# Second routed layer of a two-block network: sixteen raw slots with eight rounded halves, and identity products in three waits of TensorE

## The reference, cut to what matters

```
logits = (x @ w_router); top_val, top_idx = lax.top_k(logits, 2)
top_w = jax.nn.softmax(top_val)
for e in range(8):
    h = silu(x @ w_gate[e]) * (x @ w_up[e])          # 1024 -> 3584
    y = y + gate[..., e:e + 1] * (h @ w_down[e])     # 3584 -> 1024
```

## Time and profile before

| | |
|---|---|
| median of 3 runs | 2169.67 us (2169.33 to 2169.8) |
| profiled execution | 2166.96 us, of which the span is 2165.2 us |
| TensorE busy | 93% of the span |
| VectorE busy | 58% |
| ScalarE busy | 46% |
| DMA queue of SyncE | 571.56 MB, 69.9% of the 16 engines' span |

### The profile page before, as it was taken

How to read it: one execution, slowest core, us unless ns; L and a number is a source line. 1 busy time by engine, 2 the same in 40 slices (tenths; PEclk the granted TensorE clock), 3 DMA queues, 4 the chain that set the end, 5 groups by cost and what they waited for, 6 DMA issues and landing times.

```text
span 2165.2 us, 29319 instructions
## 1 busy us (share of the span) xinstructions
PE 2011.4 (93%) x11542; PEld 1494.7 (69%) x11542; DVE 1256.7 (58%) x1928; ACT 996.9 (46%) x1406; POOL 162.4 (8%) x151
## 2 busy tenths in 40 slices
PE   8998899999898898999989799999999999999996
PEld 7996885434497688998867676656755675575785
DVE  4557652222446677667366766646744674574797
ACT  3554442111143644443375546436644564463773
POOL 2103100000000012342000000000000000000000
PEclk9998998999999999999999989999999999999998
DMA  8650529999764125656711579999999999999994
GB/s 270 191 176 1 165 94 393 416 418 418 273 212 155 46 82 188 196 179 175 199 40 60 194 273 413 408 410 402 412 408 414 412 396 412 412 413 407 409 401 169
DMA packets 228362, 601.32 MB, mean 278 GB/s; under 512 B 16091, under 2 KB 121967, under 8 KB 205568
## 3 DMA queue, kind: packets, MB, share of 16 engines
q1 hardware_dynamic: 220112, 571.56, 69.9%
q0 software_dynamic: 8112, 27.91, 4.1%
HBM read 594.37 MB, written 5.05 MB: 277 GB/s over the span
## 4 chain that ended last, share of the span: by engine, by line
PE 70%; DMA 11%; DVE 10%; ACT 6%; issue 2%; POOL 0%; SPq 0%; DVEq 0%; ACTq 0%
PE psF L1425 8%; PE psF L1427 8%; PE psF L1426 8%; PE psB L1425 7%; PE psB L1426 7%; PE psB L1427 7%; DMA ring<-in_moe_w_up_dram 4%; PE psF L1881 4%; PE psB L2062 2%; DMA ring<-in_moe_w_gate_dram 2%; DVE ring_rounded L3486 2%; PE psB L1905 2%; DMA ring<-in_moe_w_down_dram 2%; PE psF L2062 2%; PE psB L1746 2%
## 5 line engine op out<-in xcount | busy, mean ns | idle before, releaser
L3486 DVE TENSOR_TENSOR ring_rounded<-ring,arena_rounded 128x1024 fp32r<-128x1024 f32 x296 | 350.1, 1222 | 168.2 <-ACT arena_rounded L2649 160.8
L2649 ACT ACTIVATE arena_rounded<-ring 128x1024 fp32r<-128x1024 f32 x296 | 302.6, 1057 | 196.3 <-DMA ring<-in_moe_w_gate_dram 144.0
L2926 DVE TENSOR_TENSOR ring_rounded<-ring,ring_rounded 128x2048 fp32r<-128x2048 f32 (+1 forms) x68 | 147.1, 2165 | 155.5 <-ACT ring_rounded L2376 155.3
L1426 PE MATMUL psF<-ring_rounded,arena_rounded 128*128 128x512 f32 x560 | 222.5, 397 | 0.0
L2376 ACT ACTIVATE ring_rounded<-ring 128x2048 fp32r<-128x2048 f32 (+1 forms) x71 | 128.6, 1815 | 82.1 <-PE psF L1427 62.8
L1425 PE MATMUL psF<-arena_rounded 128*128 128x512 f32 x352 | 143.6, 408 | 11.6 <-DVE ring_rounded L3486 8.5
L1427 PE MATMUL psF<-arena_rounded 128*128 128x512 f32 x352 | 140.3, 399 | 0.0
L1426 PEld LDWEIGHTS psF<-ring_rounded,arena_rounded 128*128 128x128 f32 x560 | 106.9, 191 | 22.0
L1425 PE MATMUL psB<-yT_rounded,ring_rounded 128*128 128x256 f32 x384 | 110.5, 288 | 3.8 <-DVE ring_rounded L2926 2.8
L1426 PE MATMUL psB<-memT_rounded,ring_rounded 128*128 128x256 f32 x384 | 109.2, 284 | 0.0
L1427 PE MATMUL psB<-yT_rounded,ring_rounded 128*128 128x256 f32 x384 | 109.1, 284 | 0.0
(11 more groups left out here) (577 smaller groups left out, 4836.9 us busy)
## 6 DMA issues: line engine op xcount, KB each, us to landing
ring<-in_moe_w_gate_dram SPq DMA_DIRECT2D x224, 512.0 KB, 9.0
ring<-in_moe_w_up_dram SPq DMA_DIRECT2D x224, 512.0 KB, 10.0
ring<-in_moe_w_down_dram SPq DMA_DIRECT2D x112, 1024.0 KB, 9.6
ring<-in_w_dram SPq DMA_DIRECT2D x48, 1024.0 KB, 16.4
arena<-in_w_dram SPq DMA_DIRECT2D x16, 1024.0 KB, 18.8
ring<-in_w_in_dram SPq DMA_DIRECT2D x14, 1024.0 KB, 5.4
ring<-in_ff_w_gate_dram SPq DMA_DIRECT2D x11, 1024.0 KB, 7.3
ring<-in_ff_w_up_dram SPq DMA_DIRECT2D x11, 1024.0 KB, 9.8
```

Source lines behind the costliest of these rows:

```text
L1426: mm(bank, x1, w2, start=False, stop=False, skip_group_check=open_groups)
L2649: ap_(piece(idx, w_hi).bitcast(R32), piece(idx, raw_halves), ACT.Copy).then_inc(piece_high, 1)
L2926: V.tensor_tensor(ring_r[:, slot_of[c], 0:kt * w].bitcast(R32), raw, ring_r[:, hi_slot[c], 0:kt * w], ALU.subtract).then_inc(weights_low, 1)
L3486: V.tensor_tensor(piece(idx, low_halves).bitcast(R32), piece(idx, raw_halves), piece(idx, w_hi), ALU.subtract).then_inc(piece_low, 1)
```

## The change

The ring of raw pieces gets four more half slots, in the memory of `memT` and `mv`, so 16 in all. The rounded high halves go down from 12 to 8, all in `arena`. A load waits for the piece 16 before it; the first four loads to the new slots wait for `ln8 transposed`, after which nobody reads that memory. ScalarE waits before each rounding, from the ninth big piece on, until the eighth big piece before it has been used. The new slots use four semaphores of the ordinary weight ring again, with its counts added. In three waits of TensorE at the beginning of the layer it repeats an identity product of 256 columns into bank F[3]: 4 times before the picks, 2 times before the gathered rows are saved, 6 times after they are turned.

```
-HALF_SLOTS = 2 * RING
+HALF_SLOTS = 2 * RING + 4
+HIGH_SLOTS = 8
...
+        self.big_at = [idx for idx, b in enumerate(self.pieces) if b]
...
-        raw_halves, low_halves = [ring[:, i] for i in range(RING)], [ring_r[:, i] for i in range(RING)]
+        raw_halves = [ring[:, i] for i in range(RING)] + [v[:].rearrange("p a b -> p (a b)") for v in (memT, mv)]
+        low_halves = [ring_r[:, i] for i in range(RING)] + w_hi[4:6]
...
-        piece_in = [sem(f"piece_in{i}") for i in range(HALF_SLOTS)]
+        piece_in = [sem(f"piece_in{i}") for i in range(2 * RING)] + w_in[0:4]
...
+        def landing(idx):
+
+            slot, count = order.landed[idx]
+            return piece_in[slot], count + (landed[slot - 2 * RING] if slot >= 2 * RING else 0)
...
         def piece(idx, memory):
 
+            if memory is w_hi:
+                return half_slot((order.big_no[idx] - 1) % HIGH_SLOTS, w_hi)
             return half_slot(idx % HALF_SLOTS, memory)
...
                     if idx >= HALF_SLOTS:
                         sp.wait_ge(piece_used, idx + n - HALF_SLOTS)
-                    elif idx % 2 == 0:
+                    elif idx % 2 == 0 and idx < 2 * RING:
                         sp.wait_ge(*freed[held_before[layer.first + idx // 2]])
+                    elif idx == 2 * RING:
+                        sp.wait_ge(proj_saved, saved("ln8 transposed"))
...
-                    slot, count = order.landed[idx]
-                    pe.wait_ge(piece_in[slot], count)
+                    pe.wait_ge(*landing(idx))
...
+                stay_warm(F[3], 4)
                 pe.wait_ge(tokens_halved, 1)
                 pe.wait_ge(first_picked, 1)
...
                     ins.then_inc(first_gathered, 1)
+                stay_warm(F[3], 2)
                 pe.wait_ge(first_saved, 2)
                 turn_x(0)
+                stay_warm(F[3], 6)
...
-                            slot, count = order.landed[idx]
-                            act.wait_ge(piece_in[slot], count)
+                            act.wait_ge(*landing(idx))
+                            if order.big_no[idx] > HIGH_SLOTS:
+                                act.wait_ge(piece_used, order.big_at[order.big_no[idx] - 1 - HIGH_SLOTS] + 1)
                             ap_(piece(idx, w_hi).bitcast(R32), piece(idx, raw_halves), ACT.Copy).then_inc(piece_high, 1)
```

## The result

The changed kernel takes 2157.41 us (median of 4 runs, 2152.63 to 2158.46), the kernel before on the same chip 2169.74 us. The ratio is 0.994, with an interval of 0.9923 to 0.9957. Further down, the median of eighteen slots with the changed end and those of the kernel before on its chip (2168.06) hold one slow execution each (3952 and 3344 us), which the ratios leave out.

What follows compares the result with a forecast made beforehand. The layer was taken as bound by one full stream of loads with a hole at its start. Slots (5.5 us for pair 28/29) plus products (2.8) gave 8.3 us: 2169.67 to 2161.4 us, own range 2160.6 to 2163.3, 8-in-10 range 2158 to 2166.5.

Steps and rivals of the forecast that it cites:

- the identity products: TensorE's early waits: fillers hold the clock for the gate part, gaining 2.8 us; the clock still falls after find_tokens.
- All uses come 2.8 us earlier: TensorE from piece 7 on: uses come 2.8 us earlier, so the loads gain this besides the slots' lead.
- Four more slots: SyncE's loads at the layer's beginning: four go out early, later ones wait 16 back; pair 28/29 goes 5.5 us earlier.
- The price of the products: TensorE's early waits: fillers cost nothing, 0.232 us each at full clock; even at half clock overrun at most 0.1 us.
- The gate part: TensorE, first gate part: all 48 matmuls at the faster step take 11.3 us instead of 14.2.
- Eight high halves: ScalarE's roundings: waiting for the big piece 8 back costs nothing and adds no busy time.
- The rival that ended slower: Big steps: eight halves too few, TensorE waits 2.2 us in each of 20, 2176.5 us; chance 0.08.
- Idle fillers: Layer's beginning: fillers do not hold the clock, only the slots' lead of 5.4 us remains, 2164.3 us; chance 0.18.
- Unused lead: After the beginning: TensorE can't use the stream's lead, only 2.8 us arrive, 2166.9 us; chance 0.08.
- The longer lead: Load stream's beginning: gather and loads no longer meet, or the hole nearly closes; lead 11 us, 2158.7 us; chance 0.06.
- Gaps of TensorE from too few buffers: Whole layer: twelve slots cause TensorE's 28.9 us idle, four more remove up to all of it, 2140.8 us; chance 0.02.
- The conversion to a median: Total: the runs' median lies 2.7 us above the profiled execution, so 2169.67 - 8.3 = 2161.4 us.

Runs made afterwards that it cites:

- eighteen slots with the changed end: Changed kernel with 18 raw slots, 6 high halves, no products before the gather, three at the end, VectorE's last subtractions split around the turned rows: 2152.15 us, ratio 0.9929.
- four high halves: Changed kernel with 20 raw slots and 4 high halves, ScalarE rounding four pieces, not six, ahead of the first gathered rows: 2161.42 us, ratio 0.9969.
- the mixed find_tokens: Changed kernel without identity products, the 28 narrow matmuls in four groups between gate pieces and behind the first up piece: 2160.06 us, ratio 0.996.
- products only: Kernel before, with twelve slots and twelve high halves, plus the identity products at the three places: 2162.42 us, ratio 0.9968.
- products at the end: Changed kernel plus six identity products in TensorE's wait ahead of the last down part: 2159.12 us, ratio 0.9957.
- no first products: Changed kernel without the four identity products ahead of the gather: 2158.26 us, ratio 0.9955.
- eighteen and six: Changed kernel with two of the eight high halves given to the raw slots, 18 raw and 6 high: 2153.26 us, ratio 0.994.
- slots alone: Changed kernel without the three groups of identity products, so sixteen slots and eight high halves: 2164.08 us, ratio 0.9977.

## Why the prediction was nearly right, and where it fell short

The mechanism held, and one of its terms was too small. A load issued earlier at the beginning is worth its whole time at the end: the lead of pair 28/29 and that of the last rows agree within 1.6 us in all kernels but three, which have a reason of their own (four high halves, the mixed find_tokens, the changed end), and slots and products add up. TensorE was less ahead than the stream at first and caught up by having less idle time, as forecast.

**The step that failed** is in the identity products: it was said there that `find_tokens` "still lets the clock fall after it", "and that is not removed". I had priced the products by the gate part alone, 2.8 us. That part gave 2.1 in this profile (it ends 33.96 us after the anchor for 36.07) and 2.8 in products only. But with the products the clock also stayed full through and behind `find_tokens`, and that gave 3.1 more. The use of piece 13 can be read from the load that waits for it: pair 24/25 before, 1276.29 - 1225.60 = 50.69 us after the anchor, and pair 28/29 after, 45.47. That is 5.2 us earlier, not 2.8. So the term "All uses come 2.8 us earlier" was mis-sized by 2.4 us, and the pair's lead with it: 5.5 + 5.2 = 10.7, where 5.5 + 2.8 = 8.3 was forecast. With 10.7 in the sum the forecast would have been 2159.0 us, inside the range; the last 1.6 us down to 2157.41 have no cause that a run shows, and the second measurement of the same kernel, 2160.39, lies inside the range. So that the first fell outside it is in part scatter.

Nor is the 3.1 us certain in each execution. In the second profile of the changed kernel the fall was there, if shorter, and the use of piece 13 led by 50.69 - 46.73 = 4.0:

```profile
1268.00:1272.00 4.00, 4.00 (x12) 3.19 (x11) 3.40 (x3) 0.54 (x1) 2.81 (x2) 0.58 0.38 94
```

It was there too in the kernel with products at the end, whose beginning is the same:

```profile
1268.00:1272.00 4.00, 4.00 (x14) 3.15 (x13) 2.83 (x3) 0.00 (x0) 2.25 (x2) 0.67 0.39 84
```

**Four more slots**: 5.5 forecast, 5.4 measured alone. Right.

**The price of the products** was wrong by a factor of two. "10 in 2.32 us" are five products, since each of these fp32 products is two instructions. "Even the slow case overruns by no more than 0.1 us" was therefore false for the first group: the gather began 1.1 to 1.5 us later in the profiles where that group started in time (14.40 to 14.78 us after the anchor for 13.28), and 2.3 us later in the first. How much of this reaches the gate part isn't shown; it began 0 to 0.6 us later. That a faster gather gains nothing was right: the gate part begins at 21.89 us with the gather at half clock (no first products) and at full clock (eighteen and six).

**The gate part**: begun at full clock, 11.5 us, forecast 11.3.

**Eight high halves** cost nothing that a median can show, and six left the lead of 14.2 us whole. The rival that ended slower needs 1.9 us a step; in the changed kernel ScalarE's idle time ahead of roundings that is put down to TensorE is under 4 us in the whole layer.

**The other rivals.** Idle fillers: excluded, the clock was 1.00. Unused lead: excluded by slots alone. The longer lead of 11 us has the size of what came, but not its cause: the hole didn't close (8.5 us of it are left), TensorE used pieces sooner. Gaps of TensorE from too few buffers: TensorE's idle time from 1500 to 2000 us didn't fall, 21.0 us with four more slots for 17.7 and 20.7 in the two profiles of before. It did fall before 1500, from 9.1 to 4.0 us, as TensorE took over the lead. The rule of the Trainium skill ("Perfetto Trace Analysis", section "Optimization Strategy") that the same gap repeating on the engine that should be saturated can mean too few buffers isn't borne out for TensorE by this trace: behind the full stream, at 410 GB/s in both kernels, its gaps stay.

**The conversion to a median.** The profiles say about 10 us for the change, the medians 12.3 and 8.9. That the 8.9 lies near the 8.3 forecast is luck: the lead in the profile of that time is 10.4 us. The median before was given by 3 runs that agreed within 0.5 us, and I took it for sharper than it is. What remains between 10.7 and 12.3 is within the interval of the ratio (9.3 to 16.7 us); no experiment explains it further.

## What to carry to other kernels

Where a stage runs on one full stream of loads, look first at its beginning: whatever brings the first waiting loads forward can arrive whole at the end, if no later wait gives it back (as with four high halves), and its size is (slots more, as the time between two uses) plus (how much earlier the uses come). When a filler changes an engine's clock, follow the clock through every later stretch in which it fell, not only through the one behind the filler. And count a filler's length in its own instructions before it goes into a wait.

## What the runs showed of the hardware

The granted clock fell from 1.00 to 0.50 inside a row of 28 matmuls of one column, with no idle time of TensorE in the profile. Before, the row ran from 1261.51 to 1265.36, and the windows of 1 us at 1263 and 1264 are:

```profile
1263.00:1264.00 1.00, 1.00 (x11) 1.00 (x10) 0.00 (x0) 1.00 (x2) 0.00 (x0) 0.91 0.98 340
1264.00:1265.00 1.00, 1.00 (x6) 1.00 (x6) 0.00 (x0) 1.00 (x2) 0.00 (x0) 0.50 1.03 389
```

It didn't fall there when the same 28 came in four groups between matmuls of 512 columns (two profiles, one of them without products). With identity products ahead of the gate part, in place of idle time, and the 28 in one row it stayed at 1.00 in five profiles and fell in two, for a shorter time and only about 1.2 us behind the row (0.58 and 0.67 in one window); in an eighth, with four high halves, it fell behind 1.90 us of idle time. What decides between these wasn't found. The stretch before the layer, the same in all these kernels, ended between 1223.36 and 1230.11 us in the profiled executions: 6.8 us of scatter that no part of the change can touch, more than half of what was to be measured. Counting from a row ahead of the change took it out.
